# Query projections of the next retrieval head, spread in single steps between the v tiles of four groups, with their weights loaded in two halves

## The reference, cut to what matters

```
def peer_ffn(hn, w_q, sub_keys, u_emb, v_emb):
    def block(xc):                                  # 128 tokens
        q = (xc @ w_q).reshape(T, PEER_HEADS, 2, PEER_HALF)          # 8 heads, 2 halves of 128
        s = jnp.einsum('thsd,hsnd->thsn', q, sub_keys)
        s1, i1 = lax.top_k(s[:, :, 0], 16)
        s2, i2 = lax.top_k(s[:, :, 1], 16)
        cand_s = s1[..., :, None] + s2[..., None, :]
        top_s, pos = lax.top_k(cand_s, 16); idx = ...; gate = softmax(top_s)
        act = gelu(einsum('thkd,td->thk', u_emb[idx], xc))
        return einsum('thk,thkd->td', gate * act, v_emb[idx])
```

## Time and profile before

| | us |
|---|---|
| median of 3 runs | 2320.46 |
| lowest, highest | 2319.68, 2325.69 |
| span of the profiled execution | 2319.7 |
| PE, DVE, ACT, POOL busy in it | 1812.7, 1451.5, 557.3, 1186.4 |
| share of the software DMA queue (the gathers) | 60.3% of 16 engines' span |
| PEER part | from 814 us to the end |

### The profile page before, as it was taken

The page is one execution under the profiler, slowest core; times in us unless marked ns, Lnnn a source line. Parts: engine busy times, 40 slices in busy tenths (PEclk is TensorE's granted clock), DMA queues, the critical chain, the costliest instruction groups (busy, mean ns, idle before and its releaser), DMA issues.

```text
span 2319.7 us, 23103 instructions
## 1 busy us (share of the span) xinstructions
PE 1812.7 (78%) x5927; PEld 979.2 (42%) x5927; DVE 1451.5 (63%) x2986; ACT 557.3 (24%) x1159; POOL 1186.4 (51%) x1175
## 2 busy tenths in 40 slices
PE   6778899999997828778777677767866977777677
PEld 6446435779975714333233223223322322333233
DVE  4597674443435378677666775676666766676664
ACT  2223443222332212122112211121211211121121
POOL 6970000000001065777676676765766767677774
PEclk9888899999999969999899998988998989899899
DMA  4301401334421098999998998998999899899997
GB/s 111 64 9 19 100 18 42 91 91 146 144 73 37 19 373 311 374 390 376 370 383 308 385 377 320 390 365 319 395 373 383 329 373 376 320 372 387 389 392 302
DMA packets 239397, 603.01 MB, mean 260 GB/s; under 512 B 38533, under 2 KB 105274, under 8 KB 239290
## 3 DMA queue, kind: packets, MB, share of 16 engines
q0 software_dynamic: 147840, 537.99, 60.3%
q1 hardware_dynamic: 91450, 63.85, 10.0%
HBM read 597.56 MB, written 2.10 MB: 259 GB/s over the span
## 4 chain that ended last, share of the span: by engine, by line
issue 18%; PE 15%; DMA 12%; DVE 11%; POOL 5%; DVEq 1%; ACT 1%; POOLq 0%; ACTq 0%
PE bank L1744 15%; DMA WS<-in_peer_u,R 8%; POOL R L1874 3%; DMA slabs<-in_peer_u,R 3%; POOL WS L1874 2%; DVE R L1326 1%; DVE R L1329 1%; DVE R L1327 1%; DMA R<-in_peer_v,R 1%; DVE R L1373 1%; DVE R L1328 1%; DVE R L1325 1%; POOL slabs L1874 1%; DVE H L1387 1%; DVE R L1347 0%
## 5 line engine op out<-in xcount | busy, mean ns | idle before, releaser
L1744 PE MATMUL bank<-R 128*128 128x512 f32 x2048 | 987.2, 630 | 341.1 <-ACT R L884 220.8
L1744 PEld LDWEIGHTS bank<-R 128*128 128x128 f32 x2048 | 390.4, 199 | 928.5 <-issue 673.6
L1874 POOL DMA_INDIRECT R<-in_peer_v,R x512 | 533.1, 1041 | 157.0 <-issue 142.3
L1373 DVE CUSTOM_DVE_ANT_0 R<-WS,XN 128x1024 f32<-128x1024 f32 x256 | 313.6, 1225 | 183.5 <-DMA WS<-in_peer_u,R 178.9
L1874 POOL DMA_INDIRECT slabs<-in_peer_u,R x256 | 255.8, 999 | 304.1 <-DVEq L1362 97.8
L1373 DVE CUSTOM_DVE_ANT_0 R<-slabs,XN 128x1024 f32<-128x1024 f32 x256 | 313.8, 1226 | 119.4 <-DMA slabs<-in_peer_u,R 103.3
L1874 POOL DMA_INDIRECT WS<-in_peer_u,R x256 | 252.2, 985 | 78.0 <-issue 74.3
L1869 POOL TENSOR_TENSOR FTr<-slabs,FTr 128x2048 fp32r<-128x2048 f32 x1 | 4.5, 4498 | 533.2 <-ACT FTr L626 533.2
L884 ACT ACTIVATE R<-cst,R 128x128 f32<-128x128 f32 x512 | 180.5, 394 | 355.5 <-PE bank L1744 354.5
L1471 PE MATMUL bank<-R 128*128 128x64 f32 (+5 forms) x596 | 186.5, 455 | 45.3 <-ACT R L682 20.2
L1471 PEld LDWEIGHTS bank<-R 128*128 128x128 f32 (+3 forms) x596 | 88.1, 179 | 116.5 <-issue 72.2
(11 more groups left out here) (210 smaller groups left out, 1901.8 us busy)
## 6 DMA issues: line engine op xcount, KB each, us to landing
slabs<-in_w_in SPq DMA_DIRECT2D x17, 512.0 KB, 5.3
slabs<-in_w_mem_kv SPq DMA_DIRECT2D x8, 1024.0 KB, 5.5
slabs<-in_w_peer_q SPq DMA_DIRECT2D x8, 1024.0 KB, 14.9
R<-in_peer_v,R POOLq DMA_INDIRECT x512, 6.5
slabs<-in_w_in SPq DMA_DIRECT2D x4, 1024.0 KB, 14.0
slabs<-in_w_ssm_glu SPq DMA_DIRECT2D x16, 256.0 KB, 3.2
slabs<-in_w_out SPq DMA_DIRECT2D x4, 1024.0 KB, 5.3
slabs<-in_w_mem_q SPq DMA_DIRECT2D x4, 1024.0 KB, 5.2
```

Source lines behind the costliest of these rows:

```text
L1373: dve.tensor_tensor_reduce(prod, Ub[s % URING], xn[:, t, :], 1.0, 0.0, ALU.mult, ALU.add, act_row[:, s:s + 1]).then_inc(dots, 1)
L1744: last = pe.matmul(ps[2 * (t % 2) + n][:, :], diag[s % DRING], Vb[s][:, 512 * n:512 * n + 512], start=(s == 0), stop=(s == TOPK - 1))
L1874: pool.indirect_dma_start(out=dst, out_offset=None, in_=table, in_offset=bass.IndirectOffsetOnAxis(ap=ix[:, s:s + 1], axis=0)).then_inc(si ...
```

## The change

The queries are done one step (one k, one matmul) at a time between v tiles. In the steady part, half 1 of head h+1 is done in turns t=0 (k = 0 to 3, one behind every fourth v tile) and t=1 (k = 4 to 7, behind v tiles 1, 3, 5 and 7), with the scores behind v tile 13 of t=1. Half 0 of head h+2 is done in the same way in turns t=2 and t=3 of head h, so a whole head earlier than it was. In head 0 the turns t=0 and t=1 hold both halves of head 1, one step behind each of the first 8 v tiles. ACT's `queries_out` moves behind the diagonals of turns 1 and 3 (in head 0 of turns 0, 1 and 3), ahead of the gelu. The weights come as two halves of 128 columns (512 KB, rows of 512 bytes), each with its own semaphore, issued when the half before it has been used. PE's and ACT's loops are now five passes, and head 6 is straight code; DVE's and POOL's are unchanged.

```
             with sp.Fori(1, PH) as h:
-                sp.wait_ge(q_filled, h * 2)
-                sp.dma_start(qw, w_peer_q[:, bass.ds(h * 256, 256)].rearrange("(k p) n -> p k n", p=P)).then_inc(qw_in, 16)
+                for s in range(2):
+                    sp.wait_ge(q_filled, h * 2 + (s - 1))
+                    sp.dma_start(qw[:, :, P * s:P * s + P], w_peer_q[:, bass.ds(h * 256 + P * s, P)]
+                                 .rearrange("(k p) n -> p k n", p=P)).then_inc(qw_in[s], 16)
...
+            def head(h, first=False, last=False, ahead=True):        # ScalarE
                 for t in range(NT):
                     g = h * NT + t
-                    if t < 2 and not last:
-                        queries_out(h + 1, t)
                     if not last or t < 2:
                         gate_exponentials(g + 2)
...
                         diagonals(g, t, first and t == 0)
+                    if first and t < 2:
+                        queries_out(1, t)
+                    elif t == 1 and not last:
+                        queries_out(h + 1, 1)
+                    elif t == 3 and ahead:
+                        queries_out(h + 2, 0)
                     if not last or t < NT - 1:
                         gelu_of(g + 1)
...
+            def queries(h, s, first=False, ks=range(KD)):            # TensorE
                 cols = slice(P if first else 0, T)
-                for k in range(KD):
+                for k in ks:
+                    if k == 0 and not first:
+                        pe.wait_ge(qw_in[s], h * 16)
                     ins = pe.matmul(ps[4 + s][:, cols], qw[:, k, columns(s)], FT[:, k, cols],
                                     start=(k == 0), stop=(k == KD - 1))
-                ins.then_inc(q_filled, 1)
+                    if k == KD - 1:
+                        ins.then_inc(q_filled, 1)
...
+            def beside(h, t, s, first, last, ahead):
+                if first and t < 2:
+                    if s < KD:
+                        queries(1, t, ks=[s])
+                    if s == 13:
+                        scores(1, t)
+                elif t < 2 and not last or t >= 2 and ahead:
+                    hq, sq = (h + 1, 1) if t < 2 else (h + 2, 0)
+                    if t % 2 == 0 and s % 4 == 3:
+                        queries(hq, sq, ks=[s // 4])
+                    if t % 2 == 1 and s % 2 == 1 and s < KD:
+                        queries(hq, sq, ks=[4 + s // 2])
+                    if t % 2 == 1 and s == 13:
+                        scores(hq, sq)
...
-                    last.then_inc(v_summed, 1)
+                    done.then_inc(v_summed, 1)
+                    beside(h, t, s, first, last, ahead)
```

More of the change, by code:

```diff
@@ L355, in encoder_layer @@
         mnegmax, mp_done = sem("mnegmax"), sem("mp_done")
-        qw_in, q_filled, q_copied, s_filled, s_copied = [
-            sem(n) for n in ("qw_in", "q_filled", "q_copied", "s_filled", "s_copied")]
+        qw_in = [sem(f"qw_in{s}") for s in range(2)]
+        q_filled, q_copied, s_filled, s_copied = [
+            sem(n) for n in ("q_filled", "q_copied", "s_filled", "s_copied")]
         idx_ready, gates_neg, gates_exp = [sem(n) for n in ("idx_ready", "gates_neg", "gates_exp")]
@@ L885, in diagonals @@
                                    scale=wgt[t % 2][:, s:s + 1]).then_inc(diag_done, 1)
-            def head(h, first=False, last=False):
+            def head(h, first=False, last=False, ahead=True):
                 for t in range(NT):
                     g = h * NT + t
-                    if t < 2 and not last:
-                        queries_out(h + 1, t)
                     if not last or t < 2:
@@ L914, in _ @@
             head(0, first=True)
-            with act.Fori(1, PH - 1) as h:
+            with act.Fori(1, PH - 2) as h:
                 head(h)
-            head(PH - 1, last=True)
+            head(PH - 2, ahead=False)
+            head(PH - 1, last=True, ahead=False)
             final_root(2)
@@ L1734, in scores, with group @@
                 ins.then_inc(s_filled, 1)
-            def group(g, t, taken=True):
+            def beside(h, t, s, first, last, ahead):
[12 more added lines that the diff above has]
+                        scores(hq, sq)
+            def group(h, t, first, last, ahead, taken=True):
+                g = h * NT + t
                 if taken:
@@ L1743, in group, with head @@
                     for n in range(2):
-                        last = pe.matmul(ps[2 * (t % 2) + n][:, :], diag[s % DRING], Vb[s][:, 512 * n:512 * n + 512],
+                        done = pe.matmul(ps[2 * (t % 2) + n][:, :], diag[s % DRING], Vb[s][:, 512 * n:512 * n + 512],
                                          start=(s == 0), stop=(s == TOPK - 1))
-                    last.then_inc(v_summed, 1)
-            def head(h, first=False, last=False):
+                    done.then_inc(v_summed, 1)
+                    beside(h, t, s, first, last, ahead)
+            def head(h, first=False, last=False, ahead=True):
                 for t in range(NT):
-                    if t < 2 and not last:
-                        queries(h + 1, t)
-                        scores(h + 1, t)
-                    group(h * NT + t, t, taken=not first or t >= 2)
+                    group(h, t, first, last, ahead, taken=not first or t >= 2)
             for b in range(8):
@@ L1761, in _ @@
             head(0, first=True)
-            with pe.Fori(1, PH - 1) as h:
+            with pe.Fori(1, PH - 2) as h:
                 head(h)
-            head(PH - 1, last=True)
+            head(PH - 2, ahead=False)
+            head(PH - 1, last=True, ahead=False)
         @block.gpsimd
```

3 lines of the change are left out of this document (removed).

## The result

The changed kernel takes 2335.89 us (median of 12 runs, 2331.63 to 2344.45), the kernel before 2323.69 in the same comparison (12 runs, 2317.83 to 2332.75). The ratio is 1.0056, 95% interval 1.0042 to 1.0071: slower, by about 13 us. A second comparison, further down, gave 1.0050 (1.0033 to 1.0067). I had predicted 2325, with a range of 2315 to 2335.

The account below looks back on a forecast made before the run. Gathers on the DMA engines were taken to bound PEER. The sum was 2319.7 + 2.6 + 0.8 - 1.2 + 3 = 2324.9, given as 2325 us, with an 8-in-10 range of 2315 to 2335.

Parts of the forecast that it names:

- The bound: PEER: gathers bound it at full DMA rate; t=0 is long through DVE's two fetch stalls, about 10 us in five turns.
- Steady heads, worth 0: Steady heads: moving query steps, scores and ACT's copy gains and costs nothing; all hidden, scores with 5 us of cover.
- I take +3: Weight loads, t=1 and t=3: 12 halves for 6 whole loads cost +3 us, between 0 and 4.3.
- a bound of 4.3 beneath the wider end of +16: Weight loads: +5.1 us of DMA time, scaled by 2.7 of 3.2, gives +4.3; +16 if each half costs a whole load's 2.7.
- +2.6: Head 0, t=0: gelu of group 1 at 899.5 instead of 896.80, behind last diagonal, query copy and table load.
- +0.8: Head 0, t=1: PE's scores are done at 945.1, where DVE wants them at 944.3, so +0.8 us.
- -1.2: Head 0: first half load issued at 810.7, before the gathers, lands the first u tile sooner; between 0 and -1.6 us.
- A: Halves landing late pass the turn's end into idle stretches of t=0 and t=2, saving up to 16 us: 2307; chance 0.10.
- B: Loads cost by packets, not bytes: t=3 of heads 0 to 4 goes 43.3 to 46.0, 16 us; 2338, chance 0.17.
- C: PE and ACT matter at the turn's start: 3.3 us come off t=1 in each of 6 heads; 2303, chance 0.05.
- E: Instruction fetches: ACT or PE stalls uncovered, or DVE's fetch meets a half load, a few us in five turns; 2330, chance 0.06.
- D: Whole kernel: nothing that counts changes, small terms cancel, 2320.5; inside the forecast's own range, joint chance 0.62.

Follow-up runs that it names:

- g3_head0only: Kernel before with only the change's head 0, turns t=0 and t=1; rest and loads as before: ratio 1.0010 (0.9996 to 1.0024) to the kernel before.
- g1_early: Changed kernel with whole 1 MB load, head 0 as before, scores behind tile 9 instead of 13: 2330.20 us, ratio 1.0026 to the kernel before.
- e3_head0: Changed kernel with turns t=0 and t=1 of head 0 as before, half loads kept: ratio 1.0134 to the kernel before, at the 2580 level.
- f1_spread: Changed kernel with whole 1 MB load and head 0's t=0 and t=1 as before: ratio 1.0131 to the kernel before, at the 2580 level.
- g2_after: The changed kernel run again, nothing altered: 2335.33 us against 2323.31 for the kernel before, ratio 1.0050.
- n1_noload: g1_early without the six weight loads behind the first: 2313.93 us against 2325.30 for the kernel before, ratio 0.9953.
- g4_whole: Changed kernel with a head's weights as one 1 MB load instead of two halves: 2332.75 us, ratio 1.0033 to the kernel before.

## Why the prediction was wrong

**The bound: right.** PEER's turns t=1 and t=3 last as long as their transfers (share 0.99 to 1.03 in heads 1 to 4 of all seven profiles), and t=0 of heads 2 to 6 kept its length with DVE's two stalls (53.3 to 55.4 us in the two profiles of the changed kernel, 52.0 to 54.1 before).

**Steady heads, worth 0: right for the steps in the turns, wrong for the whole.** Where all loads are out, t=1 is 216.9 for five heads, 43.4 each, and t=3 43.7, as short as turns with nothing but gathers. The steps, the late copy and the scores cost those turns nothing, and no wait of DVE for scores came up at the 2320 level. Yet the medians give this part 6.9 us with its loads. Some 2 lie in t=1, and belong to the loads, below. Most of the rest lies ahead of the first gelu, 868.9 against 863.7, and 3.7 of it ahead of the first query copy, in code that the change doesn't touch. All five profiles of spread kernels have that copy at 814.4 to 815.8, the kernel before at 810.7, and g3_head0only, which has no spreading in the steady heads, at 813.2. The time is lost in single steps of 1 to 3 us. The largest one of g1_early and of g3_head0only is the same, in the stretch from 727 to 757 us; before, g1_early, g3_head0only:

```profile
727.00:757.00 30.00, 27.34 (x173) 22.00 (x173) 11.66 (x27) 6.17 (x13) 0.00 (x0) 1.00 0.01 1
727.00:757.00 30.00, 27.44 (x146) 19.87 (x145) 9.85 (x29) 5.94 (x13) 0.00 (x0) 0.89 0.00 1
727.00:757.00 30.00, 27.45 (x151) 20.33 (x150) 9.16 (x25) 6.00 (x11) 0.00 (x0) 0.89 0.00 1
```

The clock was granted at 0.89 where it had been 1.00, so for part of the stretch it was at the lower of its two levels (1.2 GHz of 2.4), and PE did 146 and 151 matmul records in the time of 173. The changed kernel loses most of its 5 us in such steps at other moments. Of the 2580 level's profiles the spread kernels reach the copy at 809.7 to 815.5 (e3_head0 and f1_spread, with all the spreading, at 809.7 and 809.8), the others at 809.7 to 811.7, so it isn't bound to the program's text. Whether the change causes it or meets it stays open: there is one profile of each kernel and set. My sum had no term for it.

**The weight loads, "I take +3": this is the step that failed.** That rows of 512 bytes take more DMA time than their bytes is borne out. The load's queue in a t=1 of before (46.1 us) and in a t=3 of g2_after (45.2 us):

```profile
q1 hardware_dynamic: 1040, 1.05, 6.6%
q1 hardware_dynamic: 1040, 0.52, 3.9%
```

That is 3.0 us of all 16 engines for a whole load and 1.8 for a half, so 0.5 more a head for two halves. And t=3 rose by (226.6 - 218.8) / 5 = 1.6 each (I had 2.03 of DMA time and expected "about 2"). What was off is what came back in t=1. I said that it would get shorter by about 1 a head; it got shorter by (228.2 - 226.9) / 5 = 0.3. Against n1_noload the whole load of before costs t=1 (228.2 - 216.9) / 5 = 2.3, not the 2.7 that I took from the one turn in the earlier trace rows; a half costs it 2.0. So a head pays 2.0 + 1.6 = 3.6 for two halves, 1.3 more than before, and five heads 6.5 where I had 3 for all and a bound of 4.3 beneath the wider end of +16. The bound scaled both ways by 2.7 / 3.2, from one turn out of five, and assumed that a load costs the same wherever it is issued. It doesn't: the whole load costs 2.3 when it is issued 9 to 12 us into t=1 (before), 2.6 at 30 to 31 us with scores behind tile 9 (g1_early), and (235.2 - 216.9) / 5 = 3.7 there with scores behind tile 13 (g4_whole). The last is no less than the 3.6 of two halves. So the row size, for which I had reckoned the whole term, is not shown to cost these turns anything; the order in which the load now stands is. The steps and the scores alone don't do it: g4_whole's t=3 and t=1 of head 6 have both behind the same tiles and no load, and take 43.8 and 43.1. Why a load costs more beside them isn't shown. The Trainium skill (DMA: Bandwidth & Descriptors, Specifications) names 512 bytes as the least transfer for line rate. By that figure two halves would cost what one whole load costs, and in these turns, order for order, they do; the DMA time of their packets, 3.5 us against 3.0, doesn't agree.

**Head 0: right for t=0, by luck for t=1.** "+2.6" for t=0 measured 1.8 to 3.2, "+0.8" for t=1 1.6 to 2.4, alone 2.1 and 0.8. The first is the chain that I had described. The second I had put down to scores that come late, and DVE copies them without a wait; such a wait would also stand behind the gelu that ends t=1, so in t=2. What the traces have is POOL's longer wait, and a load or half that is issued 33 us into this turn where the whole one had gone at 15. The early half, "-1.2": 51.5 and 52.1 to the first gelu, against 52.8 to 54.6 in the five kernels without it, so -1.9 by the means, but those five scatter over 1.8 among themselves.

**The sum.** 2325 plus 3.5 for the loads, 1.1 for head 0, -0.7 for the early half, and 3 because the kernel before itself has a median of 2323.3 to 2323.7 over more runs and not 2320.5, is 2331.9. The 4 us that are left are as many as lie ahead of PEER, in a stretch to which I had given no term, but they can also lie in the scatter of a single profile. Taken as a difference, the forecast was +4.5 and the measured one is +12.2.

**The rivals.** A failed: the halves lay in full turns. B had the right place, t=3, and nearly the right total (2338) for the wrong reason: its price was 2.7 a half, by the number of packets, with t=1 unmoved. The trace has 1.6 and a t=1 that is 0.3 shorter, and g4_whole, with half as many packets, pays as much. C and E did not show: no turn got 3 us shorter or lost 3 us at its start, and DVE's stalls are as they were. D, no change, is outside the interval.

## What to carry to other kernels

Price a transfer that moves between turns by a mean over all turns of its kind, against a run without it, and once for each place in the turn: a difference of two single turns was off by a fifth here, and the order around the load moved its price between 2.3 and 3.7 us. Before a price is laid to the size of a transfer, run the whole one in the same order: here it cost as much as two halves. Whether a load is free where the queues stand idle was not answered. Before a table load or an activation is called hidden, look at what will stand directly ahead of it in its engine's order after the change.

## What the runs showed of the hardware

The same program took 2320 to 2325 us or 2575 to 2601, and both on one and the same chip (number 4) at different times. At the second level many semaphore hand-overs take 1.1 to 2.5 us a step, and DVE's waits for late scores 9 to 18, at a DMA share of 1.01 to 1.04. Scores that come late in a turn met no wait at the first level. At the second the changed kernel lost 1.9%, and the spread order with the whole load, without head 0's part, 1.3% (f1_spread), with six or seven such waits; no run took the waits alone away.

Granted clock over a whole run: 0.914 to 0.921 for the kernel before at the 2320 level, 0.912 to 0.919 for g3_head0only, 0.891 to 0.901 for the changed kernel, g4_whole and g1_early. Each page has the same 5,927 PE records. In the stretches above, t=1 has 1.00 with the queries in one piece (g3_head0only) and 0.88 to 0.93 with them in steps. That cost t=1 nothing in n1_noload, where it stood at 0.88 and took 43.52 us, as long as its gathers.
